# A two-layer hybrid encoder step in one kernel: the attention norm, eight conditioning products and the order of sample attention are moved

## What is computed

```python
mod = silu(c) @ w_ada + b_ada                 # 6 x 1024 values: sh1, sc1, g1, sh2, sc2, g2
u = layer_norm(x) * (1 + sc1) + sh1
q, k, v of groups A (6 heads), B (5), C (5), forget logits = split(u @ w_in)
oa, ob, oc = three kinds of attention          # widths 384, 320, 320
o = concat(group_rms(oa), group_rms(ob), group_rms(oc)) * g_out
x = layer_norm(ALPHA * x + g1 * (o @ w_out)) * ln1_g + ln1_b
u = layer_norm(x) * (1 + sc2) + sh2
x = layer_norm(ALPHA * x + g2 * (square(relu(u @ w1)) @ w2)) * ln2_g + ln2_b
```

## Time and profile before

| | us |
|---|---|
| median of 3 runs | 3370.09 (3367.11 to 3377.35) |
| profiled execution, its own time | 3378.3 |
| its span | 3376.4 |
| PE busy | 2939.2 (87%) |
| DVE busy | 1584.1 (47%) |
| POOL busy | 1511.6 (45%) |
| ACT busy | 872.0 (26%) |

### The profile page before, as it was taken

The page is one execution under the profiler, slowest core; times in us unless marked ns, Lnnn a source line. Parts: engine busy times, 40 slices in busy tenths (PEclk is TensorE's granted clock), DMA queues, the critical chain, the costliest instruction groups (busy, mean ns, idle before and its releaser), DMA issues. The chain is left out here.

```text
span 3376.4 us, 47177 instructions
## 1 busy us (share of the span) xinstructions
PE 2939.2 (87%) x18534; PEld 2794.0 (83%) x18534; DVE 1584.1 (47%) x3332; ACT 872.0 (26%) x1718; POOL 1511.6 (45%) x691
## 2 busy tenths in 40 slices
PE   6899898667599999999879989985857999999993
PEld 6899798455599999999879988973637999999992
DVE  6111887558543333333750219875585333333346
ACT  1341665314311100011123327642242000111001
POOL 2693784124254434434138838842143444343331
PEclk6999999779799999999669999986878999999996
DMA  6341211422111111110432411123211111111102
GB/s 243 98 157 37 82 46 52 149 78 81 58 51 50 37 50 50 38 49 25 193 137 98 166 49 48 47 81 106 102 63 64 50 50 37 50 50 37 50 13 115
DMA packets 118121, 256.26 MB, mean 76 GB/s; under 512 B 42692, under 2 KB 79080, under 8 KB 104468
## 3 DMA queue, kind: packets, MB, share of 16 engines
q1 hardware_dynamic: 111060, 229.11, 19.6%
q10 hardware_dynamic: 6912, 25.17, 2.2%
HBM read 219.55 MB, written 42.45 MB: 78 GB/s over the span
## 5 line engine op out<-in xcount | busy, mean ns | idle before, releaser
L370 PE MATMUL psum<-u_hi,w_hi 128*128 128x352 f32 x2016 | 653.9, 324 | 27.0 <-ACT qk_t L912 17.0
L370 PE MATMUL psum<-u_lo,w_hi 128*128 128x352 f32 x2016 | 654.5, 325 | 0.0
L370 PE MATMUL psum<-u_hi,w_lo 128*128 128x352 f32 x2016 | 653.7, 324 | 0.0
L1934 DVE SCALAR_TENSOR_TENSOR acc_t<-psum,mods,acc_t 128x704 f32<-128x704 f32 (+2 forms) x768 | 401.2, 578 | 292.7 <-PE psum L370 292.7
L370 PE MATMUL psum<-h_hi,w_lo 128*128 128x352 f32 x1536 | 495.9, 323 | 0.0
L370 PE MATMUL psum<-h_lo,w_hi 128*128 128x352 f32 x1536 | 495.5, 323 | 0.0
L370 PE MATMUL psum<-h_hi,w_hi 128*128 128x352 f32 x1536 | 494.9, 322 | 0.5 <-POOLq L353 0.5
L349 POOL CAST w_hi<-w_raw 128x2048 fp32r<-128x2048 f32 (+1 forms) x88 | 171.5, 1949 | 629.8 <-DVEq L1931 352.6
L351 POOL TENSOR_TENSOR w_lo<-w_raw,w_hi 128x2048 fp32r<-128x2048 f32 (+1 forms) x88 | 431.8, 4907 | 7.1
L370 PEld LDWEIGHTS psum<-u_hi,w_hi 128*128 128x128 f32 x2016 | 381.7, 189 | 28.2 <-issue 28.0
L1921 DVE TENSOR_TENSOR h_relu<-h_relu 128x1056 f32<-128x1056 f32 x64 | 110.9, 1733 | 619.7 <-ACT h_relu L1911 619.6
(11 more groups left out here) (247 smaller groups left out, 5433.1 us busy)
## 6 DMA issues: line engine op xcount, KB each, us to landing
w_raw<-in_w_all SPq DMA_DIRECT2D x86, 1024.0 KB, 4.8
w_ada_b<-in_w_ada_t ACTq DMA_DIRECT2D x48, 512.0 KB, 3.4
w_ada<-in_w_ada_k SPq DMA_DIRECT2D x13, 1024.0 KB, 18.2
row_tiles<-in_x_prompt SPq DMA_DIRECT2D x16, 512.0 KB, 7.4
scr_o<-o_head SPq DMA_DIRECT2D x32, 256.0 KB, 2.6
row_tiles<-scr_o SPq DMA_DIRECT2D x16, 512.0 KB, 7.6
w_ada_f<-in_w_ada_t SPq DMA_DIRECT2D x16, 512.0 KB, 3.4
x_between_norms<-row_tiles SPq DMA_DIRECT2D x16, 512.0 KB, 2.6
```

The source lines that it names most:

```text
L370: mm = pe.matmul(out[:, b, :], w[s][:, c:c + P], a[:, k, b * NB:(b + 1) * NB], start=(k == 0 and w is w_hi and a is a_hi), stop=(k == n - ...
L1934: ins = dve.scalar_tensor_tensor(a, lin[m % 2][:, b0:b1, c0:c1], mods[:, 40 + m, c:c + 1], a, ALU.mult, ALU.add)
```

## The change

Four edits, the same in both layers:

1. The attention norm. No row tile is scaled any more, but for the sample's. Three tiles of scaled identities are built, one for each group, `[128, 8, 128]`: the identity times the row's factor, for all eight prompt tiles. DVE builds those of groups A and B, POOL that of group C. PE turns a column tile by a real matmul with the scaled identity in place of a transpose with the plain one. Column tile 5 holds columns of B and of C; DVE scales its two halves itself and it is turned as before. ACT scales the sample's 32 rows in three instructions.
2. The last eight rows of `w_ada` are multiplied in the input projection: DVE does `conditions` on them, three rows ahead of the key copies, one after each of the first five key tiles. One buffer (`w_ada_v`), loaded by SP between its weight loads and its key stores. The output projection has no products, no second load of the condition vectors and no `add_bias`; the wait for the sample's gate moves to the sample's tile; the norm's gains are loaded after the third residual tile, the first MLP chunk before the row stores.
3. Sample attention takes C, B, A in place of A, B, C, and turns all keys first.
4. The MLP's accumulator isn't zeroed; the first block writes it by a scaled copy.

```diff
-                                      ("F", 0, [(0, m) for m in range(16 + ADA_B, 48)], ada_f),
+                                      ("B", 0, [(0, m) for m in range(16 + ADA_B, 48)], ada_v),
...
@@ turned_feed
+                    if turn_tiles is None:
+                        for t in range(NPT):
+                            mm = pe.transpose(wide[3][:, t * P:(t + 1) * P], x_all[:, t, k * P:(k + 1) * P], ident[:])
+                    else:
+                        mm = turn_tiles(k)
...
@@ input projection, SP
+                    sp.wait_ge(t_lo, KT + 1)
+                    sp_conditions(sp, "B", l, 0, 1)
                     sp.wait_ge(b_dve, R_STEPS)
                     sp.dma_start(scr_r[:, :], r_o[:]).then_inc(b_rout, 16)
-                    sp_weights(sp, l, 4, 2)
+                    sp_conditions(sp, "B", l, 1, 3)
+                    sp_weights(sp, l, 4, 1)
+                    sp_conditions(sp, "B", l, 3, 4)
+                    sp_weights(sp, l, 5, 1)
                     for t in range(3):
+                        sp_conditions(sp, "B", l, t + 4, t + 5)
                         store_k(t)
                     sp_weights(sp, l, 6, 1)
+                    sp_conditions(sp, "B", l, 7, 8)
...
@@ input projection, DVE
+                    conditions(own, plan_v[0:3], c_rows, ada_junk_v[:])
                     dve.wait_ge(b_rout, 16)
                     for t in range(NTT):
...
+                        if t < 5:
+                            conditions(own, plan_v[t + 3:t + 4], c_rows, ada_junk_v[:])
+                    own.settle()
+                    add_bias(own, l, 16 + ADA_B, 48, mods, None)
...
@@ sample attention, PE
+                    for g in range(4, NKT):
+                        turn_keys(g)
+                    pe.wait_ge(e_two, 1)
+                    pe.wait_ge(e_kev[0], NKT // 2)
+                    pe.wait_ge(e_kev[1], NKT // 2)
...
@@ output projection, PE
+                    def turn_scaled(k):
+                        if k in (0, 3):
+                            pe.wait_ge(f_rms_bc, 1 + k // 3)
+                        if k == 5:
+                            pe.wait_ge(f_rms_bc, 4)
+                        if k == 6:
+                            pe.wait_ge(f_rms, 1)
+                        for t in range(NPT):
+                            out, x = wide[3][:, t * P:(t + 1) * P], x_all[:, t, k * P:(k + 1) * P]
+                            if k == 5:
+                                mm = pe.transpose(out, x, ident[:])
+                            else:
+                                mm = pe.matmul(out, x, scaled_ident[k // 3][:, t, :], start=True, stop=True)
+                        return mm
...
@@ output projection, DVE
-                    for t in range(NTT):
-                        rms(t)
+                    for g in range(2):
+                        own.did(dve.tensor_tensor(scaled_ident[g][:], ident_rows, figure_columns(g, P), ALU.mult), f_rms_bc)
+                    for g, c0 in ((1, 640), (2, 704)):
+                        x = x_all[:, 0:NPT, c0:c0 + HD]
+                        own.did(dve.tensor_tensor(x, x, figure_columns(g, HD), ALU.mult), f_rms_bc)
                     own.settle()
                     split_turned_rows(own, 1, g_out, None)
-                    dve.wait_ge(f_gate, 2)
...
+                        if t == NPT:
+                            dve.wait_ge(f_gate, 2)
...
-                            conditions(own, plan[k:k + 1], c_rows_f, wide[3])
...
-                    dve.memset(acc[:], 0.0).then_inc(h_zero, 1)
+                                if isinstance(i, int) and i == 0:
+                                    ins = dve.tensor_scalar(a, y, mods[:, 40 + m, c:c + 1], None, ALU.mult)
```

More of the change, by code:

```diff
@@ L144, in build @@
         ada_prod = [at(f"ada_products{s}", Q0 + 24832 + s * 4096, [P, D]) for s in range(2)]
-        c_rows_f = at("c_rows_f", Q0, [P, 2, D])
-        ada_f = [at(f"w_ada_f{s}", W0 + s * 4096, [P, D]) for s in range(2)]
+        ada_v = [at("w_ada_v", Q0, [P, D])]
+        ada_junk_v = at("ada_products_v", Q0 + 4096, [P, D])
         row_junk = at("row_products", W0 + WB, [P, D])
@@ L170, in build @@
         ln_b = at("ln_bias", Q0 + 81920, [P, D])
+        scaled_ident = [at(f"scaled_ident{g}", o, [P, NPT, P])
+                        for g, o in enumerate((U0 + 63360, Q0 + 77824, Q0 + 81920))]
         H0 = Q0 + 42240
@@ L258, in build @@
         for stage, l, tiles, bufs in (("A", 0, [(0, m) for m in range(2 * ADA_PE[0], 16)], ada_a),
-                                      ("F", 0, [(0, m) for m in range(16 + ADA_B, 48)], ada_f),
-                                      ("F", 1, [(1, m) for m in range(16 + ADA_B, 48)], ada_f)):
+                                      ("B", 0, [(0, m) for m in range(16 + ADA_B, 48)], ada_v),
+                                      ("B", 1, [(1, m) for m in range(16 + ADA_B, 48)], ada_v)):
             plan = []
@@ L955, in _ @@
                     own.did(dve.tensor_scalar(r_o[:, 0:P - 1], r_y[:, 1:P], r_o[:, P - 1:P], None, ALU.add))
+                    own = Own(dve, dve_step)
+                    if l > 0:
+                        dve.wait_ge(b_c, 32)
+                    conditions(own, plan_v[0:3], c_rows, ada_junk_v[:])
                     dve.wait_ge(b_rout, 16)
@@ L1489, in probs @@
                         if g == "a":
-                            act.activation(esk[0:r, c], sink_two[0:r, n:n + 1], ACT.Exp, bias=nmx[0:r, c]).then_inc(e_es, 1)
+                            act.activation(esk[0:r, c], sink_two[0:r, n - FIRST_A:n - FIRST_A + 1], ACT.Exp, bias=nmx[0:r, c]).then_inc(e_es, 1)
                     def read_turned(n):
@@ L1501, in read_turned @@
                         act.activation(pt_s[n % 2][0:DEC, 16, 0:r], new, ACT.Copy).then_inc(e_ev, 1)
-                    keys_out(0)
-                    keys_out(2)
+                    for g in range(0, NKT, 2):
+                        keys_out(g)
                     for k in range(NI + 1):
-                        if k < FIRST_C:
-                            keys_out(4 + 2 * k)
                         if k < NI:
@@ L1577, in _ @@
                     dve.sem_inc(e_two, 1)
-                    keys_out(1)
-                    keys_out(3)
+                    for g in range(1, NKT, 2):
+                        keys_out(g)
                     for k in range(NI + 2):
-                        if k < FIRST_C:
-                            keys_out(5 + 2 * k)
                         if k < NI:
@@ L1697, in _ @@
                     act.wait_ge(f_figures, 1)
-                    for t in RMS_ACT:
-                        r, w = rows_of(t), GROUPS[0][1]
-                        x = x_all[0:r, t, 0:w]
-                        act.activation(x, x, ACT.Copy, scale=rsb[0:r, 4, 3 * t:3 * t + 1]).then_inc(f_rms_act, 1)
+                    for g, (c0, w) in enumerate(GROUPS):
+                        x = x_all[0:DEC, NPT, c0:c0 + w]
+                        act.activation(x, x, ACT.Copy, scale=rsb[0:DEC, 4, 3 * NPT + g:3 * NPT + g + 1]).then_inc(f_rms_act, 1)
                     read_turned_rows(act, 1, g_out, None)
@@ L1829, in _ @@
                             refine(t, 2 * k + (k < NTT), fig[0:r, 6, t:t + 1])
-                    own.settle()
-                    add_bias(own, l, 16 + ADA_B, 48, mods, None)
             LASTN = UP0 + 2 * MLP_BLK - 1
@@ L1839, in mlp, with step @@
                 up(0, UP0 % 2, UP0, 0, 0, True)
-                def step(i, par, first=False):
+                def step(i, par):
                     up(i, (UP0 + 1) % 2, 2 * i + (UP0 - 1), 10 * i - 8, par, False)
                     down(i - 1, UP0 % 2, 2 * i + UP0, 10 * i - 6, 1 - par, False)
+                step(1, 1)
                 with eng.Fori(0, (MLP_BLK - 2) // 2) as j:
                     for r in range(2):
-                        step(2 * j + (r + 1), (r + 1) % 2)
-                step(MLP_BLK - 1, (MLP_BLK - 1) % 2)
+                        step(2 * j + (r + 2), r)
                 down(MLP_BLK - 1, LASTN % 2, LASTN, 10 * MLP_BLK - 8, (MLP_BLK - 1) % 2, True)
```

74 lines of the change are left out of this document (23 added, 51 removed).

## The result

| | before | after |
|---|---|---|
| median | 3373.72 us (3367.11 to 3377.84, 4 runs) | 3323.16 us (3319.81 to 3328.12, 4 runs) |
| span of the profiled execution | 3376.4 | 3321.7 |

A forecast was written before the change was run, and what follows sets the result against it. Blocks were read one by one: PE bounds MLP and input projection, a chain of hand-overs the output projection. 48 + 10 - 18 = 40 us won gives 3338.3 profiled; the median 8.2 under, so 3330, range 3303 to 3360.

The forecast's parts named there:

- Output projection, -24 a layer: Output projection: start of row tiles, loop and tail together win 23.6, say 24 us a layer, 48 in all.
- the start of tile 1: Output projection: tile 1's sum starts at 744.4 in place of 758.72, 14.3 us won.
- the loop: Output projection, row tiles: the cycle shrinks by 0.93 to 12.2 us; seven cycles win 6.5.
- the tail: Output projection's end: `add_bias` goes and POOL's cast begins earlier, about 1.5 lost on the last `refine`s; 2.8 us won.
- Norm and turning, +3: Output projection's start: norm wins 2 us, five dearer turnings cost 5; first three tiles end at 740.1, not 737.1.
- One for one or two to one: Attention norm: how DVE and POOL take turns at the shared port; 1.3 us won or 6.4; 2 taken.
- Input projection, +9 a layer: Input projection: DVE's products push POOL; 9 us a layer lost, PE's wait before chunk 6 grows from 5.0 to 14.
- no stall of their own: Input projection, key copies behind the new waits: a round takes 10.6 us against 9.27 a key tile, without added stall.
- The rival on the key stores: Input projection: product rounds of 16 us choke the key stores, 34 us a layer lost instead of 9; 3380, chance 0.06.
- Sample attention, -10: Sample attention, both layers: 3 us won in layer 0, 7 in layer 1; ends 10 lost to 25 won.
- The rival that the C items stay slow: Sample attention: PE's clock stays at 0.55 in C items, 20 us less won in all; 3350, chance 0.15.
- Accumulator, 0: MLP: the 7.10 us of zeroing lie beside PE's work, so dropping them wins 0; 7 a layer without that cover.

The follow-up runs named there:

- e3: The changed kernel with the attention norm as before (rows scaled, plain transposes): 3324.82 us, 0.9859 of the kernel before.
- e4: The changed kernel without the eight rows' products and their loads (the MLP's gate is a constant): 3303.31 us, 0.9797 of the kernel before.
- e8: The changed kernel with 24 unread real products of the identity on PE at the output projection's end: 3320.95 us in one execution.
- e10: The changed kernel with POOL's bias addition in the output projection cut into four pieces of 256 columns: 3321.55 us, 0.9840 of the kernel before.
- e11: The changed kernel with three of refine's DVE instructions taking a column as a per-partition scalar, not a second tensor: 3305.41 us, 0.9807 of the kernel before.

## Why the prediction was right, and where it was not

- **Output projection, -24 a layer: -26.7 and -26.9.** The main thing held: tile 0's sum was held by the gate and the condition rows, not by PE. Of the terms, in layer 0, the start of tile 1 was 14.3 and is 18.8; the loop was 6.5 and is 4.6; the tail was 2.8 and is 3.3. In the loop the cycle of 12.2 was right (12.31). The first step from tile 1 to tile 2, which the forecast counted like the others, takes 13.73, because there the first `refine` of tile 1 too stands behind POOL's addition, that of tile 0 (L1820 takes 1.66 in place of 0.22).
- **Norm and turning, +3: -1.5 and 0 (e3).** This is the term of the sum that was mis-sized, and with it the start of tile 1. The price of a turning was right: seven are 16 instructions, and PE's pitch from turning to turning is 5.91 against 5.02. The norm won 3.2, not 2. What the forecast had not seen is 2.6 us won in the first column tile, since PE comes to it at the full clock.
- **One for one or two to one.** The rows fit one for one, and 3.2 were won. The sum by it, 1.3, was too low: it added 4 us of DVE's own instructions to 15.4 of POOL's, and DVE's last instruction came 17.9 after the start, 0.3 behind a POOL chain of 17.6. The Trainium skill ("SBUF — State Buffer", Who interferes with whom) says that a DVE instruction with two SBUF inputs contends with a GpSimd one that reads SBUF, and that the order of issue decides who blocks. The trace agrees: DVE's subtraction takes 4.69 beside POOL's of 4.51, and 1.23 for four times the columns at 692.15.
- **Input projection, +9 a layer: +9.1 and +11.1.** That the eight rows are the cause is shown by e4, that POOL is pushed by its busy time (11.3 more). POOL's product takes 2.57 on the mean, not 2.39. Where PE pays was half wrong: the wait before chunk 6 grows by 5.6 and 4.5, not by 9, and the rest lies at the key copies (2.1 and 2.2) and a read of PSUM (1.2 and 1.3), where the forecast had "no stall of their own". The rival on the key stores named the right place, at under a tenth of its price.
- **Sample attention, -10: -19.2.** The clock was named as the cause in layer 1 and priced at 7; the change won 11.8 there. In layer 0 it was given 3 for other reasons, and 7.4 were won, 5.9 of them in PE's busy time: PE ran under the full clock there too, though ahead of the C scores and not in them. The earlier trace rows show layer 1 alone; the whole block's clock, 0.81 in layer 0, would have shown it. The rival that the C items stay slow is refuted.
- **Accumulator, 0.** But for e8 the MLP takes 756.6 to 758.2 or 760.3 to 761.5 in these traces, before and after. In the longer form PE waits 5.9 us once at its start for DVE's split of a turned tile, behind POOL's subtraction; this comes with the zeroing (before, layer 0) and without it (after, layer 1). No run takes this edit back alone.
- **The sum.** 40 were forecast, 54.7 are the profiled difference: 9 of the 15 more are sample attention, 5.6 the output projection. That the median came within 7 us is luck in part. The forecast took 8.2 off, by which the profiled execution of before lay over its median; that of the changed kernel lies 0.3 over its own. From profile to profile 3338.3 was forecast and 3323.5 measured.

## What to carry to other kernels

Before work is moved onto an idle engine, look at whom its instructions hold: here 16 products of 1.2 us on an idle DVE cost 10 us a layer, because POOL's instructions beside them took longer (11.3 us in all) and PE waited at the end of POOL's chain. Tiny instructions on the path of a loop are worth rewriting: a column taken as a scalar of each partition in place of a second tensor won 9 us a block, more than the whole norm did. Put the long products where PE comes from gapless work, and price a block's first products by the clock that PE has when it reaches them, in every layer.

## What was not expected of the hardware

- DVE's instruction on one column each (128 x 1) waits for the end of a POOL instruction on 128 x 1024 if it reads two tensors of SBUF (1.55, e10's 0.47 to 0.66 behind pieces), and not if the second comes as a scalar of each partition (0.21 to 0.27, e11). This is shown for one column alone: DVE's cast of 128x256, which reads one tensor, took 1.29 beside POOL's cast (685.26, changed kernel), and 0.29 with POOL idle (876.71, before).
- PE's clock rose from 0.50 to 1.00 during a gapless run of 28 transposes in the changed kernel, while two runs of eight with 1.2 us between them (e3) left it at half.
- In e8 the clock, full for the first turning, was at half for the second, after waits of 1.3, 0.6 and 1.3 us with a few transposes between them.
